# Results of expert pairs added into the output rows by DMA, pairs (i, i+16), and early gates in the residual's buffer

## The reference

```
y = h + HierMoE(RMSNorm(h))        top-1 of 4 groups of 8 experts, then top-2 in the group
expert e: down_e(silu(t @ gate_e) * (t @ up_e)),  gate, up 1024 x 256, down 256 x 1024
weights: softmax over the two chosen, times the group's probability
```

## Time and profile before

| | |
|---|---|
| three runs, median (lowest, highest) | 599.04 us (596.94, 599.88) |
| the profiled execution | 603.15 us |
| its span, first to last instruction | 601.5 us |
| mean granted TensorE clock | 0.975 |
| PE busy, DVE, ACT, POOL | 552.0 us (92%), 278.9, 168.3, 156.6 |
| moved by DMA | 163.48 MB, mean 272 GB/s |
| HBM read, written | 151.06 MB, 19.76 MB |

### The profile page before, as it was taken

The page is one execution under the profiler, slowest core; times in us unless marked ns, Lnnn a source line. Parts: engine busy times, 40 slices in busy tenths (PEclk is TensorE's granted clock), DMA queues, the critical chain, the costliest instruction groups (busy, mean ns, idle before and its releaser), DMA issues.

```text
span 601.5 us, 8410 instructions
## 1 busy us (share of the span) xinstructions
PE 552.0 (92%) x2972; PEld 322.4 (54%) x2972; DVE 278.9 (46%) x694; ACT 168.3 (28%) x386; POOL 156.6 (26%) x187
## 2 busy tenths in 40 slices
PE   6999999999999989999999999999987878789993
PEld 4798899897675655553555944333332223233321
DVE  5887677978314899614458631111210111111245
ACT  7445343423302647622322210100110000000013
POOL 0488788410001187610000021121110111100003
PEclk9999999999999999999999798999998899999998
DMA  7990332589586920049805759999999999999856
GB/s 277 278 289 24 121 145 79 182 250 310 180 210 200 405 104 2 3 138 392 350 35 212 278 177 379 409 420 419 421 422 420 423 417 422 420 421 419 349 225 244
DMA packets 48199, 163.48 MB, mean 272 GB/s; under 512 B 8666, under 2 KB 22042, under 8 KB 36872
## 3 DMA queue, kind: packets, MB, share of 16 engines
q1 hardware_dynamic: 41344, 144.93, 64.1%
q0 software_dynamic: 6528, 17.01, 7.8%
q10 hardware_dynamic: 288, 1.05, 0.4%
HBM read 151.06 MB, written 19.76 MB: 284 GB/s over the span
## 4 chain that ended last, share of the span: by engine, by line
PE 47%; DMA 16%; SPq 11%; DVE 7%; issue 3%; POOL 3%; ACT 3%; DVEq 0%; POOLq 0%; ACTq 0%
PE bank L1129 10%; DMA ring<-in_w_up_dram 10%; PE bank L1061 9%; SPq L533 8%; PE bank L1156 4%; DMA x<-q_rows 3%; SPq L546 3%; DMA ring<-results 2%; PE bank L1012 2%; PE bank L831 2%; POOL ring L2188 2%; PE bank L926 2%; PE bank L809 2%; PE bank L832 2%; PE bank L836 2%
## 5 line engine op out<-in xcount | busy, mean ns | idle before, releaser
L1129 PE MATMUL bank<-ring,work 128*64 128x512 f32 x512 | 121.2, 629 | 18.3 <-DMA ring<-in_w_up_dram 18.3
L1129 PEld LDWEIGHTS bank<-ring,work 128*64 128x64 f32 x512 | 39.7, 144 | 96.5 <-issue 82.4
L1506 DVE TENSOR_TENSOR work<-work,bank 128x256 f32<-128x256 f32 x16 | 6.7, 421 | 135.1 <-ACT work L1441 135.1
L752 PE MATMUL bank<-split 128*128 128x384 f32 x192 | 66.1, 344 | 0.1
L1156 PE MATMUL bank<-ring,work 128*64 128x512 f32 x256 | 58.5, 598 | 7.6 <-ACT work L1445 7.6
L753 PE MATMUL bank<-split 128*128 128x384 f32 x192 | 64.3, 335 | 0.0
L2255 POOL DMA_INDIRECT work<-hn_rows,tbl x15 | 15.2, 1016 | 107.7 <-PE bank L1139 92.4
L1441 ACT ACTIVATE work<-bank 128x256 f32<-128x256 f32 x16 | 6.1, 384 | 131.1 <-PE bank L1129 131.1
L1061 PE MATMUL bank<-ring 128*128 128x512 f32 x96 | 42.6, 595 | 0.0
L2188 POOL TENSOR_TENSOR ring<-ring 128x192 f32<-128x192 f32 (+1 forms) x40 | 38.8, 989 | 7.9 <-DVEq L1601 6.8
L2263 POOL DMA_INDIRECT results<-work,tbl x15 | 15.0, 1001 | 99.0 <-DVE work L2033 99.0
(11 more groups left out here) (277 smaller groups left out, 873.2 us busy)
## 6 DMA issues: line engine op xcount, KB each, us to landing
ring<-in_w_down_dram SPq DMA_DIRECT2D x32, 1024.0 KB
ring<-in_w_gate_dram SPq DMA_DIRECT2D x28, 1024.0 KB
ring<-in_w_up_dram SPq DMA_DIRECT2D x28, 1024.0 KB
ring<-in_w_in_dram SPq DMA_DIRECT2D x7, 1536.0 KB, 11.3
results<-work POOLq DMA_DIRECT2D x1, 4160.0 KB, 24.5
x<-in_x_prompt_dram SPq DMA_DIRECT2D x8, 512.0 KB, 15.7
ring<-in_w_out_dram SPq DMA_DIRECT2D x2, 2048.0 KB, 16.1
ring<-in_w_gate_dram SPq DMA_DIRECT2D x8, 512.0 KB, 20.6
```

The source lines that it names most:

```text
L752: pe.matmul(bank[n % 3][:, 0:CW], xT_high[:, k, cols], w_high[c][:, k, :], start=(k == 0), stop=False)
L1129: last = pe.matmul(bank[2][64 * h:64 * h + 64, :], xgT[:, k, 64 * h:64 * h + 64], gate_up[s][h][:, :, k, :], start=(k == 0), stop=(k == KD ...
L1506: return dve.tensor_tensor(out, a, b, op)
```

## The change

The results of a pair are multiplied with their weights while they are evacuated, and the scatter adds them to the output rows in DRAM (`compute_op=ALU.add`), in two indirect DMAs: one into the 512 prompt rows, one into the 8 sample rows. For that SP stores h as the output's first value right after the projection. `weigh` now makes 16 columns, for all pairs (`slot_weight`). A scatter waits until the one before has landed. Pairs are expert i with i+16, never of one group, so that no token stands twice in a pair. `results`, its clearing, its fetching back, `holder` and the sums at the end are gone, and pair 15 is scattered as the others. Once h is stored and picked, `x` is free and takes gate and up of the first expert of pair 3 (`early_gates`); the second expert's come in halves as before.

```diff
@@ -94,8 +94,8 @@
...
-    choice = [2 * token + i for i in range(2)]
-    seg["names"] = np.stack([np.stack([token - AWAY[0]] * 2, 1), np.stack(choice, 1) - AWAY[1]], 1).reshape(P, -1)
+    decoded = np.where(token >= SEQ, token - SEQ - AWAY[1], 0)
+    seg["names"] = np.stack([np.stack([token - AWAY[0]] * 2, 1), np.stack([decoded] * 2, 1)], 1).reshape(P, -1)
...
@@ -525,18 +520,19 @@
...
-            def gates(experts, s, which=(0, 1)):
+            def gates(experts, s, which=(0, 1), where=None):
...
-                        sp.dma_start(gate_up[s][h][:, o, :, :],
+                        sp.dma_start((where or gate_up[s][h])[:, o, :, :],
...
-            def half_gates(experts, s, half, loaded):
+            def half_gates(experts, s, half, loaded, which=(0, 1)):
...
@@ -562,52 +558,45 @@
...
-                    sp.dma_start(gate_up[0][h][:, o, :, :], w[0, h].rearrange("(k p) f -> p k f", p=P)).then_inc(gu_in[0], 16)
-            downs((0, 1), 0)
-            expert(2, 3, 1)
+                    sp.dma_start(gate_up[0][h][:, o, :, :], w[0, h * PAIRS].rearrange("(k p) f -> p k f", p=P)).then_inc(gu_in[0], 16)
+            downs((0, PAIRS), 0)
+            expert(1, PAIRS + 1, 1)
...
             sp.wait_ge(S["op_done"], 4 * NT + 4)
-            gates((4, 5), 2, (1,))
+            gates((2, PAIRS + 2), 2, (1,))
+            for m, t in enumerate(ORDER):
+                sp.wait_ge(S["h_done"], m + 1)
+                sp.dma_start(y_rows[t] if t < NT else ys_rows, x[0:TILES[t], t, :]).then_inc(S["y_out"], 16)
+            sp.wait_ge(S["h_scaled"], NT + 1)
+            sp.wait_ge(S["y_out"], 16 * (NT + 1))
+            sp.wait_ge(S["xg_turned"], 2)
+            third = (3, PAIRS + 3)
+            gates(third, 0, (0,), early_gates)
             sp.wait_ge(S["pair_half"], 1)
-            half_gates((6, 7), 0, 0, gu_in[0])
+            half_gates(third, 0, 0, gu_in[0], (1,))
             sp.wait_ge(S["gu_done"], 1)
-            half_gates((6, 7), 0, 1, gu_in[0])
+            half_gates(third, 0, 1, gu_in[0], (1,))
             sp.wait_ge(S["dn_done"], 1)
-            downs((6, 7), 0)
-            expert(8, 9, 1, 4)
-            expert(10, 11, 2, 5)
+            downs(third, 0)
...
-                    expert(2 * i, 2 * i + 1, s, i)
+                    expert(i, i + PAIRS, s, i)
...
-
-            res_pairs = results.rearrange("(t k) d -> t k d", k=2)
-
-            def combine_rows(times):
-
-                sp.wait_ge(S["y_ready"], times)
-                for t in LAST:
-                    n = TILES[t]
-                    sp.dma_start(back[t][0:n], res_pairs[t * P:t * P + n]).then_inc(rows_moved[t], 16)
-                for m, t in enumerate(FINAL if times > 1 else FINAL[:NT]):
-                    sp.wait_ge(S["h_done"], times * (NT + 1) + m + 1)
-                    if times > 1:
-                        sp.wait_ge(S["y_out"], 16 * (NT + 1))
-                    sp.dma_start(y_rows[t] if t < NT else ys_rows, x[0:TILES[t], t, :]).then_inc(S["y_out"], 16)
-
-            combine_rows(1)
...
@@ -1033,7 +1020,7 @@
...
-                        last = pe.matmul(bank[7][:, 0:1], in_slot[:, i, m, :], weigh_by[:, i, m:m + 1],
+                        last = pe.matmul(bank[7][:, 0:PAIRS], in_slot[:, i, m, :], in_pair[:, i, m, :],
...
@@ -1164,42 +1151,25 @@
...
-            with pe.Fori(0, 4) as j:
+            for i in (1, 2, 3):
+                s = i % 3
+                pair(i, s, i // 3 + 1, False, False, [early_gates, gate_up[0][1]] if i == 3 else None)
+                turn_tokens(i + 1, (s + 1) % 3, 16 * (i // 3 + 1))
+                pair_down(i, s, i // 3 + 1, False)
+            with pe.Fori(0, 3) as j:
...
-            pe.wait_ge(S["slot_ready"], 5 * T5)
-            for m, t in enumerate(FINAL):
-                if t == SUMMED[1]:
-                    own_row(t, 1)
-                for half in range(2):
-                    if m == 0:
-                        pe.wait_ge(S["dn_evac_v" if half else "dn_evac_a"], PAIRS)
-                    if t == 3:
-                        pe.wait_ge(*((S["h_done"], T5 + 1) if half else (S["add_read"], 1)))
-                    pe.matmul(sum_bank(t, half)[0:TILES[t], :], holder[:, t, 0:TILES[t]], yo[0][:, half * 512:(half + 1) * 512],
-                              start=(t not in SUMMED), stop=True).then_inc(S["added"], 1)
...
@@ -1444,56 +1412,29 @@
...
-            def pair(i, s, turn, first):
+            def pair(i, s, landed, first, weight, split=False):
+
                 inner(i, first)
-                if turn is not None:
-                    act.wait_ge(res_sem[s], turn)
-                elif i == 1:
-                    act.wait_ge(S["tbl_done"], 2)
-                act.wait_ge(S["dn_done"], i + 1)
-                act.activation(yo[s][:, 0:512], bank[4][:, :], ACT.Copy).then_inc(S["dn_evac_a"], 1)
+                if landed is not None:
+                    act.wait_ge(res_sem[s], landed)
+                else:
+                    act.wait_ge(S["tbl_ready"], 4)
+                if split:
+                    act.wait_ge(S["pair_half"], 2)
+                else:
+                    act.wait_ge(S["dn_done"], i + 1)
+                act.activation(yo[s][:, 0:512], bank[4][:, :], ACT.Copy, scale=weight).then_inc(S["dn_evac_a"], 1)
...
-            def weighted_row(half):
-
-                cols = slice(half * 512, (half + 1) * 512)
-                act.activation(yo[0][:, cols], bank[4 + half][:, :], ACT.Copy, scale=last_weight)\
-                    .then_inc(S["dn_evac_v" if half else "dn_evac_a"], 1)
...
-            act.wait_ge(res_sem[0], 80)
-            act.wait_ge(S["act_done"], PAIRS)
-            act.wait_ge(S["pair_half"], 2)
-            weighted_row(0)
-            act.wait_ge(S["dn_done"], PAIRS)
-            weighted_row(1)
-            for t in SUMMED:
-                for half in range(2):
-                    for i in range(2):
-                        scaled_rows(t, i, slice(half * 512, (half + 1) * 512))
-            act.wait_ge(S["h_done"], 2 * T5)
-            act.dma_start(y_rows[FINAL[-1]], x[:, FINAL[-1], :]).then_inc(S["y_out"], 16)
+            for i in range(PAIRS):
+                pair(i, i % 3, 32 * (i // 3) if i >= 3 else None, i == 0, slot_weight[:, i:i + 1], i == PAIRS - 1)
...
@@ -2016,7 +1956,7 @@
...
-            tt(weigh_by, in_pair[:, :, :, PAIRS - 1], w12, ALU.mult).then_inc(S["tbl_ready"], 1)
+            tt(in_pair, in_pair, bc(w12, 3, PAIRS, [P, 2, T5, PAIRS]), ALU.mult).then_inc(S["tbl_ready"], 1)
...
@@ -2026,71 +1966,22 @@
...
-            def result(i, s, turn):
-                if turn is not None:
-                    dve.wait_ge(res_sem[s], turn)
+            def result(i, s, landed, weight):
+
+                if landed is not None:
...
                 dve.wait_ge(S["dn_done"], i + 1)
-                dve.tensor_copy(yo[s][:, 512:D], bank[5][:, :]).then_inc(S["dn_evac_v"], 1)
-
-            for i in range(4):
+                dve.tensor_scalar(yo[s][:, 512:D], bank[5][:, :], weight, None, ALU.mult).then_inc(S["dn_evac_v"], 1)
+
+            for i in range(PAIRS):
                 hidden(i, i == 0)
...
                 if i == 0:
                     dve.wait_ge(S["tbl_done"], 2)
-                    dve.tensor_copy(last_weight, bank[7][:, 0:1])
...
-            def add_rows(t):
-
-                dve.wait_ge(rows_moved[t], 32)
-                need(put(add_row(t, 0)))
-                return add_row(t, 1)
...
+                    dve.tensor_copy(slot_weight, bank[7][:, 0:PAIRS]).then_inc(S["tbl_ready"], 1)
+                    dve.wait_ge(S["tbl_ready"], 4)
+                result(i, i % 3, 32 * (i // 3) if i >= 3 else None, slot_weight[:, i:i + 1])
...
@@ -2212,16 +2097,6 @@
...
-            def clear_results(times):
-
-                pool.wait_ge(S["zero_rows"], times + 1)
-                pool.dma_start(results.rearrange("(a b) d -> a b d", a=80), bc(xg[0][0:80, :], 1, 13, [80, 13, D]))\
-                    .then_inc(S["scattered"], 16)
-
-            pool.wait_ge(S["v_used"], 2)
-            pool.memset(xg[0], 0.0).then_inc(S["zero_rows"], 1)
-            clear_results(1)
...
@@ -2255,40 +2130,44 @@
...
-            def scatter(i, s, choices):
+            def add_rows(s, tokens, decoded):
+
+                for out, at, n in ((y_prompt[0], tokens, SEQ), (ys_rows, decoded, DEC)):
+                    pool.indirect_dma_start(out, bass.IndirectOffsetOnAxis(at, 0), yo[s], None, bounds_check=n - 1,
+                                            oob_is_err=False, compute_op=ALU.add).then_inc(res_sem[s], 16)
+
+            def scatter(i, s):
 
                 pool.wait_ge(S["dn_evac_a"], i + 1)
                 pool.wait_ge(S["dn_evac_v"], i + 1)
+                if i >= 1:
+                    pool.wait_ge(res_sem[(i - 1) % 3], 32 * ((i - 1) // 3 + 1))
                 pool.sem_inc(S["moved_go"], 1)
-                pool.indirect_dma_start(results, bass.IndirectOffsetOnAxis(choices, 0), yo[s], None,
```

(29 more changed lines are left out.)

174 lines of the change are left out of this document (58 added, 116 removed).

## The result

| | before | changed |
|---|---|---|
| median of 4 runs each (lowest, highest) | 599.46 us (596.94, 600.23) | 604.91 us (603.48, 605.72) |
| profiled execution, span | 603.15, 601.5 | 603.48, 601.8 |
| mean granted TensorE clock in it | 0.975 | 0.966 |

The ratio is 1.0114 (95% interval 1.0076 to 1.0152) and the medians differ by 5.45 us: slower, against the 1.8 of the forecast. The two profiled executions differ by only 0.3 us, because before's was 3.7 us above its median and the changed kernel's was the lowest of its four. So the traces are read in stretches, and the sum is made against the medians.

The account below looks back on a forecast made before the run. Bound after 372 us by bytes through 16 DMA engines: tail -10.7, added read +10, second DMA +1.5, start +1.0 sum to +1.8 on the 599.0 us median, 600.8 us; own range 595 to 607, full range 588 to 615.

Parts of the forecast that it names:

- Tail: After the last down load: fetching back and sums go, leaving 13.3 us in place of 23.96, -10.7 us.
- The added read: Saturated stretch from 372 us: each adding scatter also reads the output row, +10 us, bounds 0 and +20.5.
- terms 2 and 3: Saturated stretch: the add's extra read, +10 us, and the second DMA per pair, +1.5 us; break-even at 9.7 together.
- The second DMA: Each pair's extra scatter for the 8 sample rows, nearly all small packets: +1.5 us, bounds 0.5 and 4.
- Start: Start of the expert stage: early loads gain nothing, first gather slowed by full queues, PE slips 0 to 2.4: +1.0 us.
- point 5: Parts priced at nothing, among them the clearing at 189 us that goes, as PE is busy there anyway.
- At nothing: Evacuation factor, waits between scatters, removed clearing at 189 us and new expert pairing were to cost or gain nothing.
- the signs: Stretch 10 to 13 us longer, q0 share about 17%, end 13 us after last down load, pair 4's loads near 372.05.
- D: Rival: queue still full at 372 us, so pair 3's earlier loads save up to 5 us, 595.8 us; chance 0.05.
- A: Rival: the add's read is hidden beside other work, so only the tail counts, 590.3 us; chance 0.20.
- B: Rival: in the saturated stretch an added row costs more than two plain ones, 611.3 or 618.7 us; chance 0.27.
- C: Rival: scatters landing over 12.4 us late stop POOL ahead of gathers, 13 us per us, 612 us; chance 0.03.

Follow-up runs that it names:

- e7: Changed kernel with POOL reading its flag early and SP instead of POOL waiting for the last scatters: 601.17 us, ratio 1.0022 to before.
- e1: Changed kernel with scatters writing instead of adding, so output rows are wrong: 591.67 us, ratio 0.9871 to before.
- e2: Changed kernel without the second scatter of each pair, into the 8 sample rows, whose results are missing: 603.86 us, ratio 1.0106 to before.
- e3: Changed kernel with POOL reading the flag and taking the branch before it waits for the last scatters: 602.58 us, ratio 1.0090 to before.
- e5: Changed kernel with an expert's rows spread over its 64 slots' partitions instead of filling from the first: 601.33 us, ratio 1.0024 to before.
- e6: Kernel before with an expert's rows spread over the partitions by the same permuted constant: 597.39 us, ratio 0.9958 to before.
- e10: Changed kernel with rows spread over the partitions, POOL's flag read early and SP waiting for the last scatters: 596.73 us, ratio 0.9954 to before.
- e8: Kernel before with the clearing of the result rows issued behind the arrival of the output projection's weights: 598.08 us, ratio 0.9978 to before.
- e4: Changed kernel with the early gates undone, pair 3's gate and up loaded in halves behind pair 0 again: 606.36 us, ratio 1.0105 to before.

## Why the prediction was right or wrong

**The sign and the range held, by terms of which one was wrong by 7.6 us.** That 604.91 us lies within 595 to 607 owes much to luck: errors of 4.2 us the other way made up for more than half of it. The point of the forecast, 600.8, was no change, and the result is not within its 596.0 to 602.0; slower had a chance of 0.42.

1. *Tail: forecast -10.7, measured -3.1. This is the step that failed.* Of its parts, from the evacuation's end to POOL's issue 0.84 was forecast and 588.63 - 587.79 = 0.84 came. Too small were: the down matmuls (3.65 forecast, 4.87 came, at a clock of 0.75 between 582 and 587 us, after PE had stood still for most of 577.5 to 581; this is the execution's, for e7 stood still as long and had 3.65, as e1, e2 and e3); the issue (0.97 forecast, 1.55 came); and above all the way from the second issue to the end. "For an add on nearly idle engines I take 5.0", and 0.8 for the flag: 5.8 forecast, 11.3 came. (In all 1.5 us for the matmuls, 0.6 for the first issue and 5.5 for this way.) The last packets were gone 4.0 us after the issue began, so the 5.0 was near for the landing; the 7.3 us behind it, from the last packets to the end of a program in which POOL waits, were priced with 0.8, one instruction of DVE's. e3 and e7 take 4.0 of them away without touching any transfer; what the other 3.3 are isn't known. No row of before showed this time, since POOL was done there long before the end; its last store shows only what SP and ACT need, 4.3 us from the issue to the end at 601.5, of which a store takes 2.2:

```profile
597.24 0.38 ACTq L1490 DMA_DIRECT2D out_dram<-x  x1
```

2. *The added read: forecast +10, measured 11.8 by e1 with the second DMA's adds in it (terms 2 and 3 together 11.5).* The mean engine was forecast at 8.6 + 1.5 = 10.1 and paid 484 - 289 = 195 engine-us, 12.2 us, of which some 2 filled gaps (the share rose from 0.98 between 372 and 577 us to 0.99). That is because a row pays 0.19 more, not 0.158, and because 14 scatters of the saturated stretch count, not 13. The other half of the step, that the slowest engine pays 1.36 times the mean, wasn't borne out: the lag is 6.2 us, where before had 6.5. Two errors of 2 us cancelled. That the lag itself comes from the rows' partitions held for the changed kernel (e5), and was not shown for before (e6).

3. *The second DMA: forecast +1.5;* measured 0.9 (plain, e1 against before) to 1.4 (adding, against e2), and no difference in the medians.

4. *Start: forecast +1.0, measured -2.0.* In this profile PE did not slip: no wait of its stage names the tokens. In e1, e5 and e10 it did, by 1.5 to 2.0 us, as the term has it (0 to 2.4). Of the clearing point 5 says that it "lets w_out land earlier, but PE is busy 24.6 of 25 us there"; the work behind those 25 us does wait for w_out, and the projection starts 2.0 us earlier (e8, by way of POOL, which begins on w_out 8.8 us earlier). The early gates: nothing gained that a run could show, as forecast, though e4 leaves 4 us open.

5. *At nothing: held, but for the clearing.* PE's waits in the whole stage of the changed kernel name the weights and ACT's hidden rows, 7.1 us as in before; none names evacuations, tokens or a scatter:

```profile
PE bank L1116 <- DMA ring<-in_w_up_dram: 28.0, 8, 5.8
PE bank L1143 <- ACT work L1413: 7.1, 15, 0.5
PE bank L1134 <- DMA ring<-in_w_down_dram: 2.4, 1, 2.4
```

Those for the gate and up loads grew from 18.3 us to 28.0, by 9.7 of the 10.3 us of the stretch.

Sum: the forecast +1.8, off by +7.6 (tail), -3.0 (start and clearing) and -1.2 (stretch: 10.3 measured against 11.5) gives +5.2; the medians say +5.45.

Of the signs, the longer stretch at fewer GB/s (385) came. q0's share was 14.0% and not 17%, which doesn't follow from the forecast's own terms: 289 + 16 x 10.1 engine-us in 216 us are 13%. The end came 20.9 us after the last down load and not 13, and pair 4's loads 6.9 us earlier and not within 2.4, with no gap in the DMA ahead of them (see D below).

**The rivals.** A (the read is hidden) fell: e1 shows 11.8 us of it. B (a row costs more than two) was met in kind, 2.2 rows instead of 2, but far from the 0.377 on which its 611 rested. Terms 2 and 3 together measured 10.3 to 11.8, over the 9.7 at which the change was to break even, and about what the forecast had; that it is slower by more than the forecast is the tail's doing. C (scatters become a chain) is half true. POOL's waits between 365 and 581 us:

```profile
POOL out_dram L2136 <- DMA out_dram<-work,tbl: 39.6, 6, 7.6
```

Six times a scatter stood for the landing of the one before. But no buffer or gather came late for PE by it, and e2, with half the scatters, keeps the stretch. D (early loads shorten the stage) stays open. Its condition, a queue still full when pair 4's loads come, was met in the changed kernel:

```profile
362.00:366.00 4.00, 4.00 (x24) 1.65 (x20) 0.43 (x2) 0.38 (x1) 1.52 (x1) 1.00 1.02 393
```

The share is 0.97 or more in every 2 us from 360 to 372 there, and in e2, e3, e7 and e8, all with the full clock between 335 and 345 us; the gap on which the forecast went is one of the lowered clock (0.39 from 370 to 372 us in e1). What the early gates are worth at the full clock was not measured apart.

## What to carry to other kernels

A DMA that adds into DRAM cost a bit over two plain rows on the engines here (a factor of 2.2); where these are the bound, nearly all of it is paid (11.2 us per engine, 10 to 11.8 of time), and a read-back saved at the end has to be larger than the sum over all scatters. Price the end of a program from its last issue to the last instruction, the landing and the waiting engine's way out included, and try another engine for the waiting (SP instead of POOL gave 2.7 us). Compare medians, or profiles with the same clock, and not one pair of profiles: two executions of one kernel were 4 us and more apart. Where gathered or scattered rows fill a fixed slot range unevenly, look at the DMA share of the last 20 us: spreading them over the partitions gave about 5 us in the changed kernel and some 2.5 in before, for one changed constant.

## What the runs showed of the hardware that was not expected

- An adding indirect DMA holds POOL for 1.55 us, a plain one for 0.97, with the same rows.
- On nearly idle engines the last packet of an adding scatter moved up to 4.0 us after its issue began (590.49 to before 594.5), that of a plain one up to 2.3 (581.73 to before 584, e1).
- Behind the last packets the program needed 7.3 us where POOL waited and then read the flag (7.6 with plain scatters, e1), 6.4 where POOL had read it before (e3), and 3.3 to 3.7 where SP waited (e10, e7).
- Kernels that do the same up to there had PE at a granted clock of 1.00 or of 0.66 to 0.71 between 335 and 345 us, busy 10.00 of 10 us in either (changed kernel and before; 9.78 in e7, at 1.00). What PE did before doesn't tell them apart: in e4 it was busy 5.00 of 5 us up to 333 us at 1.00, as in the changed kernel, and was at 0.50 (1.2 GHz) from 336 to 339. The cause isn't known.
- The clearing of 4.26 MB at 189 us held up the projection, which begins 68 us later without it (256.94, e8), by 2.0 us.
